# Sample pages loaded in the order of the transposes: three transfers for each page in place of one, and GpSimd's sorting copies left out

## What is computed

```python
PAST_LEN, PAGE_SIZE, DEC_BATCH = 1024, 128, 8
# cache_kv (DEPTH, N_PHYS, PAGE_SIZE, 4, NSA_KV_HEADS, HEAD_DIM): paged rows [k_cmp, v_cmp, k_sel, v_sel]
past_kv = cache_kv[l][page_table].reshape(bd, past_rows, 4, NSA_KV_HEADS, HEAD_DIM)

def compress_blocks(rows, pe, w1, w2):
    b, length = rows.shape[:2]
    n_cmp = (length - CMP_BLOCK) // CMP_STRIDE + 1
    idx = jnp.arange(n_cmp)[:, None] * CMP_STRIDE + jnp.arange(CMP_BLOCK)[None, :]
    blocks = jnp.take(rows, idx, axis=1) + pe[:, None, :]
    flat = blocks.transpose(0, 1, 3, 2, 4).reshape(b, n_cmp, NSA_KV_HEADS, CMP_BLOCK * HEAD_DIM)
    return jax.nn.silu(flat @ w1) @ w2

k_cmp = compress_blocks(kv_all[:, :, 0], pe[0], w1[0], w2[0])   # first quarter of a row
v_cmp = compress_blocks(kv_all[:, :, 1], pe[1], w1[1], w2[1])   # second quarter
```

## Time and profile before

| what | value |
|---|---|
| median of 3 executions | 3989.98 us (3989.86 to 3991.4) |
| profiled execution: its time | 3985.85 us |
| profiled execution: span from first to last instruction | 3984.1 us |
| PE busy | 3807.4 us, 96% of the span |
| PE weight loads (PEld) | 3487.8 us, 88% |
| DVE busy | 2006.2 us, 50% |
| GpSimd (POOL) busy | 1701.1 us, 43% |
| ACT busy | 1124.3 us, 28% |
| DMA | 349.62 MB, mean 88 GB/s |

### The profile page before, as it was taken

How to read it: one execution, slowest core, us unless ns; L and a number is a source line. 1 busy time by engine, 2 the same in 40 slices (tenths; PEclk the granted TensorE clock), 3 DMA queues, 4 the chain that set the end, 5 groups by cost and what they waited for, 6 DMA issues and landing times. The chain is left out here.

```text
span 3984.1 us, 83564 instructions
## 1 busy us (share of the span) xinstructions
PE 3807.4 (96%) x34199; PEld 3487.8 (88%) x34199; DVE 2006.2 (50%) x4501; ACT 1124.3 (28%) x2486; POOL 1701.1 (43%) x2284
## 2 busy tenths in 40 slices
PE   8998999989999999999999989999899999999998
PEld 8987788866699999999999877888665999999998
DVE  6587544457545414414556874444574454144153
ACT  3154233347731000100212532333477210000012
POOL 5633222136754434434355421222377644344342
PEclk9998999999999999999999999999999999999998
DMA  4255433220042131131323554332200411311313
GB/s 131 85 163 168 130 88 87 70 97 7 13 124 66 43 127 54 43 138 40 113 93 92 162 172 107 85 88 71 96 9 12 139 54 45 136 43 57 124 39 99
DMA packets 204334, 349.62 MB, mean 88 GB/s; under 512 B 73410, under 2 KB 138050, under 8 KB 203074
## 3 DMA queue, kind: packets, MB, share of 16 engines
q1 hardware_dynamic: 203954, 344.29, 27.7%
HBM read 253.03 MB, written 95.90 MB: 88 GB/s over the span
## 5 line engine op out<-in xcount | busy, mean ns | idle before, releaser
L2644 POOL CAST wr_hi<-wr_raw 128x256 fp32r<-128x256 f32 x584 | 262.8, 450 | 894.3 <-PE ps L2680 888.8
L2646 POOL TENSOR_TENSOR wr_lo<-wr_raw,wr_hi 128x256 fp32r<-128x256 f32 x584 | 548.6, 939 | 46.7
L2680 PE MATMUL ps<-xh,wr_hi 128*128 128x384 f32 x2064 | 453.7, 328 | 0.0
L2680 PE MATMUL ps<-xh,wr_lo 128*128 128x384 f32 x2064 | 453.1, 327 | 0.0
L2680 PE MATMUL ps<-xl,wr_hi 128*128 128x384 f32 x2064 | 452.9, 327 | 0.0
L1409 POOL TENSOR_TENSOR rc_CT<-rc_AT,rc_masks 128x256 f32<-128x256 f32 x192 | 135.6, 724 | 527.6 <-DVE rc_AT L1444 409.3
L2747 ACT ACTIVATE de_c<-de_c 128x1088 f32<-128x1088 f32 (+1 forms) x44 | 49.1, 1116 | 1098.1 <-DVE de_c L2857 1098.1
L2680 PEld LDWEIGHTS ps<-xh,wr_hi 128*128 128x128 f32 x2064 | 348.9, 188 | 0.3
L2680 PEld LDWEIGHTS ps<-xl,wr_hi 128*128 128x128 f32 x2064 | 349.0, 188 | 0.0
L2680 PEld LDWEIGHTS ps<-xh,wr_lo 128*128 128x128 f32 x2064 | 348.7, 188 | 0.0
L2680 PE MATMUL ps<-de_mixh,wr_hi 128*128 128x384 f32 (+1 forms) x1440 | 317.8, 329 | 8.1 <-DVE de_mixl L2782 8.1
(11 more groups left out here) (453 smaller groups left out, 7555.2 us busy)
## 6 DMA issues: line engine op xcount, KB each, us to landing
sa_kvp<-in_cache SPq DMA_DIRECT2D x128, 256.0 KB
scr_xres<-de_x SPq DMA_DIRECT2D x56, 544.0 KB, 2.7
de_x<-scr_xres SPq DMA_DIRECT2D x56, 544.0 KB, 3.6
wr_raw<-in_w_gate SPq DMA_DIRECT2D x42, 512.0 KB, 3.6
wr_raw<-in_w_up SPq DMA_DIRECT2D x42, 512.0 KB, 3.7
rc_arbk<-scr_arbk SPq DMA_DIRECT2D x32, 512.0 KB, 4.7
wr_raw<-in_w_down SPq DMA_DIRECT2D x32, 512.0 KB, 3.6
pr_raw<-in_w_rw SPq DMA_DIRECT2D x28, 512.0 KB, 4.4
```

The source lines that it names most:

```text
L2644: pool.tensor_copy(hi[:, k, :], raw[:, k, :]).then_inc(w_hi, 1)
L2646: pool.tensor_tensor(lo[:, k, :], raw[:, k, :], f32(hi[:, k, :]), ALU.subtract).then_inc(w_ready, 1)
L2680: m = pe.matmul(ps[:, (bank + b) * BANK:(bank + b) * BANK + cols], w[:, k, :], x[:, k, o:o + cols], start=(k == 0 and i == 0), stop=(k == ...
```

## The change

The order that the copies made is now made by the transfers. A page comes in three transfers: one for the compressed half of the even rows and one for that of the odd rows (each 64 partitions x 4 pieces of 64 numbers, so 256 bytes a piece on the side of the tile, with a gap of 256 bytes between them), and one for the selected halves (64 partitions x 2 pieces of 1 KB). `sa_kvp` so holds 512 sorted numbers, then 512 of the selected halves. GpSimd's copies, their tile and the semaphore `sorted` are gone. PE waits for `row_in` itself and transposes out of `sa_kvp`. The prompt's rows (b = 8) are loaded in twelve transfers in place of four. The place of the old tile in memory stays as an unused gap (`sa_gap`), so all other tiles lie where they were.

```diff
-ROWS_IN = 16 * (PAGES + 3)
+ROWS_IN = 16 * (3 * PAGES + 3)
...
             if b == NB:
                 for n in range(4):
-                    sp.dma_start(kvp2[:, u, n, :], kvrows[l, n * 256:(n + 1) * 256, :].rearrange("(p e) n -> p (e n)", e=2)).then_inc(row_in[u], 16)
+                    rows = kvrows[l, n * 256:(n + 1) * 256, :].rearrange("(p e) (a x) -> p e a x", e=2, a=2)
+                    for e in range(2):
+                        sp.dma_start(kvp2[:, u, n, 0:512].rearrange("p (x e d) -> p e x d", e=2, d=HD)[:, e], rows[:, e, 0].rearrange("p (x d) -> p x d", d=HD)).then_inc(row_in[u], 16)
+                    sp.dma_start(kvp2[:, u, n, 512:1024].rearrange("p (e x) -> p e x", e=2), rows[:, :, 1]).then_inc(row_in[u], 16)
                 return
             for p in range(PAGES):
                 page = sp.value_load(ptab[0:1, b * PAGES + p:b * PAGES + p + 1], min_val=0, max_val=NPHYS - 1)
-                sp.dma_start(kvp2[64 * (p % 2):64 * (p % 2) + 64, u, p // 2, :], cache[l, page]).then_inc(row_in[u], 16)
+                rows, to = cache[l, page].rearrange("p (e a x) -> p e a x", e=2, a=2), kvp2[64 * (p % 2):64 * (p % 2) + 64, u, p // 2, :]
+                for e in range(2):
+                    sp.dma_start(to[:, 0:512].rearrange("p (x e d) -> p e x d", e=2, d=HD)[:, e], rows[:, e, 0].rearrange("p (x d) -> p x d", d=HD)).then_inc(row_in[u], 16)
+                sp.dma_start(to[:, 512:1024].rearrange("p (e x) -> p e x", e=2), rows[:, :, 1]).then_inc(row_in[u], 16)
...
-                        pe.wait_ge(sorted_, c + 1)
+                        pe.wait_ge(row_in[u], ROWS_IN * (c // 2 + 1) if c < NB else ROWS_IN * (NB // 2) + 192)
...
-                            m = pe.transpose(ps[:, o:o + P], kvc[:, n, kg, :], cst["ident"])
+                            m = pe.transpose(ps[:, o:o + P], kvp[:, n, kg * P:(kg + 1) * P], cst["ident"])
...
         def sample_pool(pool):
-            def sort_rows(c):
-                pool.wait_ge(row_in[c % 2], ROWS_IN * (c // 2 + 1) if c < NB else ROWS_IN * (NB // 2) + 64)
-                if c:
-                    pool.wait_ge(k_turned, 2 * c)
-                else:
-                    pool.wait_ge(e_st_done, 4)
-                for n in range(4):
-                    m = pool.tensor_copy(...)
-                m.then_inc(sorted_, 1)
...
+            for n in range(SAMPLE_STEPS):
+                yield
```

More of the change, by code:

```diff
@@ L932, in scan_with_samples @@
                   "u_top u_bottom st_done s_added s_ready out_done out_copied rows_kept y_kept")
-    sample_names = ("row_in0 row_in1 sorted q_sorted cm_in gates_in prepared weighed bias_done bias_kept k_turned k_even k_odd hidden hid_ready sel_turned "
+    sample_names = ("row_in0 row_in1 q_sorted cm_in gates_in prepared weighed bias_done bias_kept k_turned k_even k_odd hidden hid_ready sel_turned "
                     "win_turned c_made kc_kept ks_kept kw_kept c_scored w_scored s_scored c_maxed c_exp c_ready imp_ready w_masked "
@@ L948, in scan_with_samples @@
          u_top, u_bottom, st_done, s_added, s_ready, out_done, out_copied, rows_kept, y_kept) = scan_sems
-        (row_in0, row_in1, sorted_, q_sorted, cm_in, gates_in, prepared, weighed, bias_done, bias_kept, k_turned, k_even, k_odd, hidden, hid_ready, sel_turned,
+        (row_in0, row_in1, q_sorted, cm_in, gates_in, prepared, weighed, bias_done, bias_kept, k_turned, k_even, k_odd, hidden, hid_ready, sel_turned,
          win_turned, c_made, kc_kept, ks_kept, kw_kept, c_scored, w_scored, s_scored, c_maxed, c_exp, c_ready, imp_ready, w_masked,
@@ L958, in scan_with_samples @@
         region = sc.sb("sc_region", [P, 13600])
-        kvp2, kvc, kt, ksT, wT = sc.place(base, (("sa_kvp", [P, 2, 4, 1024]), ("sa_kvc", [P, 4, 4, P]), ("sa_kt", [P, 4, 8, 64]), ("sa_ksT", [P, 2, 512]), ("sa_wT", [P, 272])))
+        kvp2, _, kt, ksT, wT = sc.place(base, (("sa_kvp", [P, 2, 4, 1024]), ("sa_gap", [P, 4, 4, P]), ("sa_kt", [P, 4, 8, 64]), ("sa_ksT", [P, 2, 512]), ("sa_wT", [P, 272])))
         (_, _, eG, eAT, eCT, eXX, eys, ep1, ebkr, eUV, eGV, eyo, eAM, eS8, emasks) = sc.place(base, (
@@ L1556, in sample_tensor @@
                             o = (4 + e) * BANK + n * P
-                            m = pe.transpose(ps[:, o:o + P], kvp[:, n, e * 512 + 256:e * 512 + 384], cst["ident"])
+                            m = pe.transpose(ps[:, o:o + P], kvp[:, n, 512 + e * 256:512 + e * 256 + 128], cst["ident"])
                         m.then_inc(sel_turned, 1)
@@ L1629, in sample_tensor @@
                     for g in range(2):
-                        pe.matmul(oo[g], pT[:, n, 32 * g:32 * g + 32], kvp[:, pp, e * 512 + 384 + g * HD:e * 512 + 384 + (g + 1) * HD], start=(n == 0), stop=False)
+                        pe.matmul(oo[g], pT[:, n, 32 * g:32 * g + 32], kvp[:, pp, 640 + e * 256 + g * HD:640 + e * 256 + (g + 1) * HD], start=(n == 0), stop=False)
                 for g in range(2):
@@ L1809, in sample_pool @@
         def sample_pool(pool):
-            def sort_rows(c):
-                pool.wait_ge(row_in[c % 2], ROWS_IN * (c // 2 + 1) if c < NB else ROWS_IN * (NB // 2) + 64)
-                if c:
-                    pool.wait_ge(k_turned, 2 * c)
-                else:
-                    pool.wait_ge(e_st_done, 4)
-                for n in range(4):
-                    m = pool.tensor_copy(kvc[:, n].rearrange("p kg (e d) -> p e kg d", e=2),
-                                         kvp2[:, c % 2, n].rearrange("p (e a kg d) -> p e a kg d", e=2, a=2, kg=4)[:, :, 0])
-                m.then_inc(sorted_, 1)
             pool.tensor_copy(qs[:, :, :].rearrange("p b (r t) -> p b r t", r=R4),
                              qT[:, :, SEQ:NT].rearrange("p r (b t) -> p b r t", b=NB)).then_inc(q_sorted, 1)
-            for n in range(4):
+            for n in range(SAMPLE_STEPS):
                 yield
[L1825 to L1834, removed]
         @block.sync
```

## The result

The changed kernel takes 4009.97 us (median of 6 runs, 4004.26 to 4016.39), the kernel before 3989.92 us on the same occasion (median of 6, 3987.61 to 3991.4). The ratio is 1.0052, with a 95% interval from 1.0041 to 1.0064: slower by half a per cent, 20 us. The forecast was 4007 us with a range of 4000 to 4017.

The account below looks back on a forecast made before the run. PE, 96% busy, was taken as the bound. Round 0 waits of +16.8 us plus 1 us of clock on 3985.85 gave 4003.6; the median's 4.1 made 4007.8, rounded to 4007 us, range 4000 to 4017.

Parts of the forecast that it names:

- The bound and the place: PE bounds the stage; the loss falls on its first transposes in round 0 of each layer, +16.8 us together.
- The added issues: Sixteen more SyncE issues ahead of round 0's rows, 0.67 us each (0.51 to 0.80), 10.8 us a layer.
- the number of pieces does not set the issue time: Step for SyncE's new transfers: four pieces a partition issue in the same 0.469 us as one piece.
- the signs given for being right: In each layer PE's first transposes wait 9 to 12 us; page issues take about 20 us in place of 9.13.
- The gain from the sort: Sorting copies leave round 0's path before PE's transposes: 2.48 and 2.33 us, a gain of 4.8 us.
- The release behind the loads: SyncE's release of the copies to sa_kt comes 10.8 us later; cost taken as zero, at most 1 us a layer.
- The clock: PE's longer round 0 wait prolongs its half clock: 0.5 us a layer, together +1, between nothing and 1.7 each.
- the rest of the stage keeps its length: Sign of being right: outside round 0's wait the stage takes as long as before.
- (a): Rival: transfers of 256-byte pieces, not issues, set round 0's landing; +28 us, 4017 us; chance 0.10.
- (b): Rival: SyncE's extra issues are hidden and round 0's path is only shortened; -5 us, 3985 us; chance 0.08.
- (c): Rival: SyncE becomes the bound in every round through stalled issues; +70 us and more, 4080 us; chance 0.05.

Follow-up runs that it names:

- round0_old: The changed kernel with round 0 of each layer put back to one transfer a page and GpSimd's sort: 3990.67 us, ratio 0.9999 to the kernel before.
- later_old: The changed kernel with only rounds 1 to 8 put back to one transfer a page and GpSimd's sort: 4009.8 us, ratio 1.0053.
- order_left_out: The changed kernel with as many transfers, but compressed halves laid in 1 KB pieces, even/odd order left out: 4007.42 us, ratio 1.0045.
- numbers_first_old: The kernel before, sort kept, with round 0's page numbers read ahead of SyncE's wait for the chunk's outputs: 3982.49 us, ratio 0.9982.

## Why the prediction was right

**The bound and the place** held. PE's wait at the first transposes accounts for the change: 19.7 us of waits against 20 us of time, no wait on rows in rounds 1 to 8, and no gain to be seen from POOL's freed 41.7 us. round0_old and later_old show it from both sides, and over all nine kernels the time of each moved as its waits did, to within 6 us. That the two numbers agree to 0.3 us is chance: the waits come from one execution, and kernels with the same round 0 had 4.6 and 7.1 us, or 24.3 and 28.1.

**The added issues** were mis-sized. I took 0.67 us each, with 0.80 as the upper end, on the reading that "the number of pieces does not set the issue time". This step failed: (2.87 - 1.24)/2 is 0.81 us, just outside of my range. For the page transfers the runs show 0.469 us with one piece a partition, 0.547 to 0.556 with two and 0.599 with four. So the signs given for being right were passed a little too: a first wait of 12.35 us where it was to be 9 to 12, and 23.1 us of page issues (438.74 - 415.63) where about 20 were expected. The row that I leaned on was not of the kind: rc_vT with 0.437 us has its four pieces on the side of memory and lies in one piece in the tile, and the new transfers have theirs in the tile. It is not the register address that sets the new ones apart. The prompt's rows (b = 8) are loaded without one, and their issue grew too, from 0.432 us in one piece in the kernel before to 0.602 with four in the tile:

```profile
L1032 SPq DMA_DIRECT2D sa_kvp<-out_kvrows x8: 431/432/1917, 767.7 to 2747.9; - x8
```

```profile
L1034 SPq DMA_DIRECT2D sa_kvp<-out_kvrows x16: 502/602/2064, 782.0 to 2780.4; - x16
```

Whether the side of the pieces is what matters stays open: the third transfer of a page has its two pieces on the side of memory only, and costs 0.547 all the same. In all the chain from the first issue to sa_wn grew by 14.0 us (24.25 - 10.27) in the first layer and by 12.7 in the second, not by 10.8: sixteen times 0.81 is 13.0, and single issues of up to 1.3 us come on top of it in the first layer.

**The gain from the sort**, 2.4 us a layer, held, and one thing came to its help that I had put at nothing: the last transfer lands sooner after its issue, 2.4 us (442.29 - 439.88) in place of 3.2, with the DMA engines less loaded. So 14.0 - 2.5 - 0.8 = 10.7 us, which is the growth of the first wait, 12.35 - 1.72 = 10.6. In the second layer it lands 1.2 us sooner, 2.3 in place of 3.5, and 12.7 - 2.3 - 1.2 = 9.2 stands beside 11.98 - 2.92 = 9.1. The sum was 16.8 us for both layers, measured 19.7: the issues were 5.1 us dearer than I had them, and the landing gave back 2.0. That these errors point in opposite directions is luck. With the landing as before, the waits would have stood at 21.7 us, above the 20.8 of my upper end for them, though the range for the whole would still have held them.

**The release behind the loads** came close to its end: ACT's first copy into sa_kt starts at 445.19, its wait ended by SyncE, and PE's product follows 6.25 us after the transposes began (448.54 - 442.29), where it was 5.9.

**The clock.** After the long wait PE runs at 1.2 GHz for its first transposes: 1.97 us for the first group at 442.29, where it was 1.51 in the earlier trace rows, with a granted clock of 0.50:

```profile
442.00:446.00 4.00, 3.71 (x37) 3.26 (x39) 0.79 (x2) 0.59 (x1) 0.00 (x0) 0.50 0.66 249
```

I had put 1 us on this for both layers. Beside the waits it cost about that: from the first group of transposes to the second it takes 4.43 us (446.72 - 442.29) in place of 4.24 in the first layer, and 4.63 (2443.27 - 2438.64) in place of 4.08 in the second, 0.7 us together. The profiled execution lost more elsewhere: its time stands 30.5 us above the profiled one of before, 19.7 of it in the two waits. Part of the rest lies in rounds 1 and 2, where the granted clock falls in places where it had been full, so for this execution the sign "the rest of the stage keeps its length" did not hold. One such stretch in the changed kernel, and the same work in the kernel before:

```profile
495.00:546.00 51.00, 49.24 (x794) 43.25 (x789) 21.44 (x66) 17.03 (x40) 9.95 (x14) 0.93 0.32 86
```

```profile
483.00:532.00 49.00, 46.58 (x788) 40.64 (x784) 20.79 (x66) 16.64 (x40) 12.08 (x18) 1.00 0.33 89
```

The same work takes 2 us longer at 0.93. This differs from run to run: among the six runs of the changed kernel those with a mean granted clock of 0.979 have spans of 4002.5, 4003.2 and 4006.7 us, those with 0.974 to 0.976 have 4009.7 to 4014.6. What brings these falls in a given run stays open; no experiment was aimed at it. The profiled one was the slowest of the six, and that of the kernel before was faster than all six timed beside the change.

**The rivals.** (a), the pieces of 256 bytes set the landing: fell with order_left_out and with the DMA share of 0.38. Behind it stood a row of the Trainium skill ("DMA: Bandwidth & Descriptors", Specifications), which gives 512 bytes as the least transfer for line rate; I had read it as a rule for each piece. Whatever that rate is, these engines had room for it, and the measured pieces cost SyncE 0.13 us a transfer and no landing time. The same page advises to coalesce many small transfers into one large one ("Rules for kernel authors"), and there the trace agrees: three transfers need 2.87 us of SyncE for a page where one needed 1.24. (b), the extra issues are hidden: fell, since each costs 0.71 to 0.81 us in the chain. (c), SyncE bounds every round: fell. Single issues of up to 2.1 us do occur, but the last issue of the load of round 2 is at 523.08, and PE starts on its rows at 546.07. Three slips of the prediction changed nothing: its 4007.8 us rounds to 4008; (a)'s +28 us gives 4018; and the trace has issues below 0.3 us, that of sa_wn with 0.28.

## What to carry to other kernels

A transfer that is reshaped to save another engine's copies can cost the issuing queue, and the price must be read where nothing covers it: here in round 0 of each layer, not in the steady rounds. Before splitting transfers, count the issues between the event that frees the buffer and the last landing, at the price of the same kind of transfer (pieces a partition, and on which side they lie). What is independent of the event, such as reading page numbers, should stand ahead of the wait; here that alone gained 0.18% (0.05 to 0.30) on the kernel before, and together with issuing from a second queue it repaired the changed one. Once the issues are quick enough, look at the landing of the last transfer: in numbers_first_old it took back most of what the shorter chain had gained in the first layer.

## What the runs showed of the hardware that was not expected

The time that SyncE takes to issue a transfer grows with its pattern: for the page transfers, whose address comes out of a register, from 0.469 us with one piece a partition over 0.547 with two to 0.599 with four. Each is the median of 128 to 384 issues; none lies more than a nanosecond below it, and single ones reach 1.8 us. Reading a page number costs 0.58 us of SyncE's pitch, about as much as the issue of a transfer. How long the last transfer of a load takes to land goes with the DMA share while the load runs: 2.2 to 2.5 us at 0.35 to 0.43, 3.2 to 4.0 us at 0.73 to 0.77 and 6.3 to 6.5 us at 0.91 to 0.96. A chain of issues that is made longer so gives a little back at its end, and one that is made shorter gains less than it saves.
